# Seven products for eight in 24 pairs of feed-forward weight blocks, with two ring slots split by one instruction there

## The reference, cut to what matters

```python
x = x + (jax.nn.silu(hf @ w_gate[layer]) * (hf @ w_up[layer])) @ w_down[layer]
...
h2 = rms_norm_2(x, g_ffn[i])
x = x + (jax.nn.silu(h2 @ w_gate[i]) * (h2 @ w_up[i])) @ w_down[i]
```

## Time and profile before

| | |
|---|---|
| median of 3 runs | 2388.45 us (2387.97 to 2388.83) |
| the profiled execution: its time / its span | 2390.59 us / 2388.8 us |
| busy: TensorE, VectorE, ScalarE, GpSimd | 100%, 72%, 48%, 1% of the span |
| granted TensorE clock, mean | 0.999 |
| DMA engines | 58.9% of 16 engines' span, 193 GB/s |

### The profile page before, as it was taken

How to read it: one execution, slowest core, us unless ns; L and a number is a source line. 1 busy time by engine, 2 the same in 40 slices (tenths; PEclk the granted TensorE clock), 3 DMA queues, 4 the chain that set the end, 5 groups by cost and what they waited for, 6 DMA issues and landing times.

```text
span 2388.8 us, 31593 instructions
## 1 busy us (share of the span) xinstructions
PE 2380.6 (100%) x10836; PEld 1983.8 (83%) x10836; DVE 1727.6 (72%) x2386; ACT 1145.1 (48%) x1561; POOL 12.8 (1%) x26
## 2 busy tenths in 40 slices
PE   9999999999999999999999999999999999999999
PEld 7988888888888888888888888888888888888887
DVE  7798887876567656668897977977656765666885
ACT  6554555644444434445554445454444443444553
POOL 1000000000000000000000000000000000000000
PEclk9999999999999999999999999999999999999999
DMA  8655555556565665556555564565655565565655
GB/s 294 240 176 185 167 168 175 187 188 207 189 198 178 208 194 189 198 177 196 187 191 200 180 213 161 193 202 187 208 188 199 178 209 193 189 197 180 206 191 168
DMA packets 126859, 461.97 MB, mean 193 GB/s; under 512 B 14096, under 2 KB 14736, under 8 KB 126112
## 3 DMA queue, kind: packets, MB, share of 16 engines
q1 hardware_dynamic: 123648, 446.49, 56.7%
q0 software_dynamic: 2816, 13.68, 1.7%
q10 hardware_dynamic: 288, 0.33, 0.0%
HBM read 458.35 MB, written 2.10 MB: 193 GB/s over the span
## 4 chain that ended last, share of the span: by engine, by line
PE 99%; ACT 0%; DMA 0%; DVE 0%; issue 0%; SPq 0%; DVEq 0%
PE acc L479 94%; PE acc L758 1%; PE acc L484 1%; PE po L741 1%; PE acc L672 1%; PE po L733 1%; PE pt L712 0%; PE acc L687 0%; PE acc L516 0%; PE pt L568 0%; DMA heads<-mem_in 0%; PE acc L657 0%; PE acc L694 0%; ACT tmp_a L1084 0%; PE po L516 0%; ACT tmp_b L1084 0%
## 5 line engine op out<-in xcount | busy, mean ns | idle before, releaser
L1364 DVE TENSOR_TENSOR w_lo<-raw,w_hi 128x1024 fp32r<-128x1024 f32 x844 | 1025.7, 1224 | 580.5 <-ACT w_hi L913 573.0
L913 ACT ACTIVATE w_hi<-raw 128x1024 fp32r<-128x1024 f32 x843 | 890.3, 1060 | 1028.7 <-PE acc L479 951.7
L479 PE MATMUL acc<-w_hi,norm_hi 128*128 128x512 f32 (+1 forms) x2228 | 867.2, 389 | 0.1
L479 PE MATMUL acc<-w_hi,norm_lo 128*128 128x512 f32 (+1 forms) x2228 | 864.0, 388 | 0.0
L479 PE MATMUL acc<-w_lo,norm_hi 128*128 128x512 f32 (+1 forms) x2228 | 592.7, 388 | 0.0
L479 PEld LDWEIGHTS acc<-w_hi,norm_hi 128*128 128x128 f32 x2228 | 418.3, 188 | 85.8 <-issue 0.8
L479 PEld LDWEIGHTS acc<-w_hi,norm_lo 128*128 128x128 f32 x2228 | 418.3, 188 | 85.0
L479 PEld LDWEIGHTS acc<-w_lo,norm_hi 128*128 128x128 f32 x2228 | 417.1, 188 | 85.8
L479 PE MATMUL acc<-w_hi,mix_hi 128*128 128x512 f32 x1088 | 424.7, 390 | 1.9 <-ACT w_hi L1162 1.9
L479 PE MATMUL acc<-w_hi,mix_lo 128*128 128x512 f32 x1088 | 423.8, 390 | 0.0
L479 PE MATMUL acc<-w_lo,mix_hi 128*128 128x512 f32 x1088 | 291.6, 390 | 0.0
(11 more groups left out here) (235 smaller groups left out, 912.9 us busy)
## 6 DMA issues: line engine op xcount, KB each, us to landing
raw<-stream SPq DMA_DIRECT2D x843, 512.0 KB, 4.2
heads<-x_in POOLq DMA_DIRECT2D x4, 512.0 KB, 9.2
x<-x_tok POOLq DMA_DIRECT2D x4, 512.0 KB, 7.4
x<-mem_tok POOLq DMA_DIRECT2D x2, 1024.0 KB, 6.9
x<-x_tok POOLq DMA_DIRECT2D x1, 2048.0 KB, 9.7
heads<-rows_in POOLq DMA_DIRECT2D x2, 1024.0 KB, 8.4
heads<-decay_in POOLq DMA_DIRECT2D x4, 512.0 KB, 5.2
heads<-mem_in SPq DMA_DIRECT2D x3, 512.0 KB, 7.4
```

The source lines that it names most:

```text
L479: last = pe.matmul(acc[:, slot, c * NB:c * NB + width], a[:, k * T + c * P:k * T + (c + 1) * P], w[:, s, kk * width:(kk + 1) * width], sta ...
L913: act.activation(w_hi[:, (units.fixed - 1) % RING, :], src, ACT.Copy).then_inc(w_hi_ready, 1)
L1364: dve.tensor_tensor(w_lo[:, s, :], src, w_hi[:, s, :].bitcast(F32), ALU.subtract)\
```

## The change

In a 2 x 2 product of tiles (two chunks of the contraction by two token tiles, times two chunks by two blocks of columns) seven tile products and some sums take the place of eight (Winograd's form). The change does this for the **first unit of each of the two blocks** of a pair, in 12 pairs of each network: up pair 3 of group 1, all up pairs of groups 2 and 3, the second down pair of group 1, both of group 2. The pairs are numbered j = 0 to 11 in this order of work: group 1: up 3 (0), down 2 (1); group 2: up 1 to 4 (2 to 5), down 1, 2 (6, 7); group 3: up 1 to 4 (8 to 11). The two units leave the stream (48 of 844) and come instead as one 1 MB transfer each from `seven_in`, issued by GpSimd into `heads`.

- VectorE makes three combined weight tiles and one more (`seven_sums`, four subtractions of 512 columns, two of which are waited for), ScalarE rounds four and then three tiles (`seven_hi`, 2048 and 1536 columns), VectorE writes their low parts (`seven_lo`).
- TensorE runs four of the products (`open_seven`, 12 matmuls) inside the second block of the pair before, and three (`close_seven`, 9 matmuls) at the start of the pair; then 7 units per block where there were 8 (5 for 6, 7 for 8 in down pairs). Between the two ScalarE copies one quarter out (`first_out`) and one back (`third_in`), and VectorE adds quarters in PSUM (`combine`, four additions of 512 columns).
- The same sums of activation tiles are made once per network for `norm` and once per group for `mix` (`sums_raw`, `sums_hi`, `sums_lo`).
- For a pair with seven products two blocks use PSUM of `pt` and `po` in some pairs (`banks_at`).
- In `mlp`, outside the last group's down pairs, VectorE's `split` takes two neighbouring slots in one instruction (`split_two`) where the first is even and no other work stands between.
- The hardware loops are written out.

```diff
+            def split_two():
+                raws.add(2)
+                dve.wait_ge(w_hi_ready, units.add(2))
+                s = (units.fixed - 2) % RING
+                dst, src, hi = (t[:, s:s + 2, :].rearrange("p s n -> p (s n)") for t in (w_lo, raw, w_hi))
+                dve.tensor_tensor(dst, src, hi.bitcast(F32), ALU.subtract).then_inc(raw_read, 2)
...
+            def seven_hi(j, part):
+                first, n = ((W11, 4), (W22, 3))[part]
+                if part == 0:
+                    act.wait_ge(seven_summed, j + 1)
+                act.activation(hi7(first, n), raw7(first, n), ACT.Copy).then_inc(seven_hi_ready, 1)
...
+            def open_seven(j, act, ready):
+                c11, c12, c21, c22 = quarters_of(j)
+                pe.wait_ge(block_taken, first_of(j) - 2)
+                pe.wait_ge(seven_ready, 2 * j + 1)
+                pe.wait_ge(act_ready, sums_needed(j))
+                products(j, ((c11, "a11", W11), (c22, "s1", T1), (c12, "s2", T2), (c21, "s3", T3)), act, ready, True)\
+                    .then_inc(products_done, 1)
+            def close_seven(j, act, ready):
+                c11, c12, c21, c22 = quarters_of(j)
+                pe.wait_ge(seven_ready, 2 * j + 2)
+                pe.wait_ge(combined, j + 1)
+                pe.wait_ge(third_copied, j + 1)
+                products(j, ((c11, "a21", W21), (c12, "s4", W22), (c21, "a22", T4)), act, ready, False)\
+                    .then_inc(seven_used, 1)
...
+            def seven_sums(j):
+                dve.wait_ge(seven_landed, 16 * (j + 1))
+                dve.tensor_tensor(raw7(T3), raw7(W22), raw7(T1), ALU.subtract)
+                link(dve.tensor_tensor(raw7(T1), raw7(T1), raw7(W11), ALU.subtract))
+                link(dve.tensor_tensor(raw7(T2), raw7(W22), raw7(T1), ALU.subtract))
+                dve.tensor_tensor(raw7(T4), raw7(W21), raw7(T2), ALU.subtract).then_inc(seven_summed, 1)
...
+            def combine(j):
+                c11, c12, c21, c22 = quarters_of(j)
+                dve.wait_ge(first_copied, j + 1)
+                link(dve.tensor_tensor(u_second, u_first, c12, ALU.add))
+                dve.tensor_tensor(u_third, u_second, c21, ALU.add).then_inc(third_summed, 1)
+                dve.tensor_tensor(c12, u_second, c22, ALU.add)
+                dve.wait_ge(third_summed, j + 1)
+                dve.tensor_tensor(c22, u_third, c22, ALU.add).then_inc(combined, 1)
...
+            for j in range(N_SEVEN):
+                if j:
+                    pool.wait_ge(seven_used, j)
+                else:
+                    pool.wait_ge(w_used, U_MLP_AT[0] + 2)
+                load_seven(j)
```

More of the change, by code:

```diff
@@ new lines, in mlp @@
+                    for p in range(n):
+                        pair = g, "up", p
+                        j, after = (seventh(which, q) for q in all_pairs[all_pairs.index(pair):][:2])
+                        early = {4: [lambda: hidden_hi(p - 1)]} if p else {}
+                        if (g, p) == (0, 0):
+                            during(2 * NU - 3, at)
+                            wait_rows()
+                            gated()
+                            split(3)
+                            taken.add()
+                            continue
+                        if j is None:
+                            sums = {5: [lambda: sums_hi(which, False)], NU - 1: [gated]}
+                            steps(2 * NU, both(early, sums, preparing(after, 6), joining(after, 13)))
+                        else:
+                            sums = {10: [lambda: sums_hi(which, True)]} if p == 2 and g < LAST_GROUP else {}
+                            if after is None and g < LAST_GROUP:
+                                after_ = seventh(which, (g, "down", 1))
+                                ready_ = {}
+                            else:
+                                after_, ready_ = after, joining(after, 11)
+                            steps(2 * NU - 2, both(early, preparing(after_, 5), {NU - 2: [gated]}, sums, ready_))
+                        taken.add()
@@ new lines, in mlp @@
+                    if g == LAST_GROUP:
+                        break
+                    for p in range(2):
+                        pair = g, "down", p
+                        j, after = (seventh(which, q) for q in all_pairs[all_pairs.index(pair):][:2])
+                        turned_ = {3 if j is not None else 4: [lambda: hidden_hi(n - 1)]} if p == 0 else {}
+                        if j is None:
+                            steps(2 * nd, both(turned_, joining(after, 9)))
+                        else:
+                            steps(2 * nd - 2, both(turned_, preparing(after, 6 if p == 0 else 5),
+                                                   joining(after, 2 * nd - 5 if nd > 6 else 9)))
+                        taken.add(2)
@@ L1342, in _ @@
         def _(dve):
-            raws, units, ends, taken, his, squared, sums, roots_n, funcs, rows, own, evicted, roped, moved = (
-                Tally() for _ in range(14))
+            raws, units, ends, taken, his, squared, sums, roots_n, funcs, rows, own, evicted, roped, moved, sums_made = (
+                Tally() for _ in range(15))
             def link(ins):
@@ new lines, in mlp, with steps, preparing, joining @@
+            def mlp(name, next_name, at, which, final=False, beside=None):
+                all_pairs = list(FIRST_BLOCK)
+                def steps(n, then):
+                    by_two[0] = True
+                    done = 0
+                    for at_ in [*sorted(then), n]:
+                        split(at_ - done)
+                        done = at_
+                        for do in then.get(at_, ()):
+                            do()
+                    by_two[0] = False
+                def preparing(j, at):
+                    if j is None:
+                        return {}
+                    return {at: [lambda: seven_sums(j)], at + 3: [lambda: seven_lo(j, 0)],
+                            at + 4: [lambda: seven_lo(j, 1)]}
+                def joining(j, at):
+                    return {} if j is None else {at: [lambda: combine(j)]}
+                def both(*parts):
+                    out_ = {}
+                    for part in parts:
+                        for k, do in part.items():
+                            out_[k] = out_.get(k, []) + do
+                    return out_
@@ new lines, in mlp @@
+                for b in range(NBD):
+                    if b:
+                        if final:
+                            dve.wait_ge(final_ready, b)
+                        rows_ = by_tile(block_of(heads, Y // CB + b - 1)) if final else x_of(b - 1)
+                        for quarter in range(4):
+                            split(1)
+                            turned = turn_quarters(tmp_c[:, :], by_row(rows_), (quarter,))
+                        turned.then_inc(x_turned, 1)
+                        if beside and b == NBD - 1:
+                            beside()
```

479 lines of the change are left out of this document (320 added, 159 removed).

## The result

| | before | after |
|---|---|---|
| time, median | 2388.64 us (2387.97 to 2389.14) | 2427.45 us (2425.69 to 2428.85) |
| ratio to before, 95% interval | | 1.0162 (1.0145 to 1.018) |
| matmuls | 10836 | 10764 |
| TensorE / VectorE busy | 100% / 72% | 98% / 77% |
| network 1, network 2 (TensorE's units, first to last) | 732 / 922 us | 751 / 942 us |

The account below looks back on a forecast made before the run. TensorE, busy 2380.6 of 2388.8 us, was taken as the bound. From the profiled execution, 2390.59 - 16.3 (matmuls saved) + 45 (new waits) = 2419.3, or 2417 us as a median; range 2386 to 2440.

Parts of the forecast that it names:

- What is saved: TensorE, 24 pairs with 21 matmuls where there were 24: 72 x 0.2267 = 16.3 us less, median 2372.1 with no new wait.
- The opening in a common pair: Before `open_seven`, TensorE waits for `seven_lo` 1.20 us, 1.35 with the weight load, at five pairs per network.
- The closing: Before `close_seven`, TensorE waits for `combine` 0.76 us, 0.91 with the load, at seven pairs per network.
- The uncommon places: Three per network: opening of j = 2 waits 4.36 us, its closing 2.55, opening of j = 7 2.5.
- The sum of the waits: All openings, closings and uncommon places: TensorE waits 22.5 us per network, 45 us for both.
- The price of the pieces: Added VectorE and ScalarE instructions, priced from profile rows: `seven_sums` 2.72 us, `combine` 2.63, `seven_hi` 1.84 and 1.40, `seven_lo` 2.22.
- the likeliest case: TensorE's waits as worked out around the products, with their bounds: median 2401 to 2433 us, chance 0.65.
- The rival with the clock: TensorE falls to its lower clock behind six long waits: up to 10 us more, 2427; chance 0.13 together with a late load.
- The rival of the late load: `seven_in` lands over 15.5 us after issue, delaying 14 openings: 3 us late is 2459; chance 0.13 together with lower clock.
- The rival that the added work fits: Added VectorE and ScalarE pieces fit between TensorE's fixed points: 2379 if 40% shorter, 2372 with no waits; chance 0.16.
- What would show it: TensorE idle per network 12 to 16 us before `open_seven`, about 9 before `close_seven`; ScalarE waiting at `seven_hi`; VectorE about 80% busy.

Follow-up runs that it names:

- experiment 1: The change with VectorE's low halves made one slot at a time again, seven products kept: 2403.73 us, ratio 1.0069 to the kernel before.
- experiment 3: The change with one slot per instruction only in the low-half steps directly ahead of `combine`: 2412.54 us, ratio 1.0106 to the kernel before.
- experiment 8: The kernel of experiment 7 with the two-slot low halves put back: 2396.54 us, ratio 1.0034 to the kernel before.
- experiment 2: The change with the opening products one unit later in up pairs that themselves go by seven products: 2415.88 us, ratio 1.0113 to the kernel before.
- experiment 4: The change with sums of weights, first-quarter copy and combination one slot earlier in the second pair of group 1's down projection: 2410.79 us, ratio 1.0093.
- experiment 5: The change with four more linked subtractions of 512 columns on VectorE ahead of each preparation of weights: 2516.26 us, ratio 1.0536 to the kernel before.
- experiment 7: The change with the edits of experiment 1, experiment 2 and experiment 4 together: 2375.20 us, ratio 0.9947 to the kernel before.
- experiment 10: The kernel of experiment 7 with the three products of each tile in another order, first two matmuls sharing an operand: 2374.57 us, ratio 0.9941.
- experiment 9: The kernel of experiment 7 with one or two TensorE waits less ahead of each group of products: 2375.42 us, ratio 0.9948.

## Why the prediction was right, point by point

- **What is saved.** 72 matmuls less (10836 to 10764) at 0.2267 us. The kernels with next to no waits (0.8 and 2.2 us) take 2373.15 and 2375.20 us where 2372.1 was worked out for none.
- **The opening in a common pair.** Forecast 1.35 us, five per network; measured 1.36 ten times over, 1.20 of it idle, at the places that were named. The 0.15 us that I took for the weight load is 0.16.
- **The closing.** Forecast 0.91, seven per network; measured 0.90, at the seven places that were named. That the wide split ahead of `combine` causes it was argued there and is shown by experiments 1, 3 and 8.
- **The uncommon places.** j = 2: forecast 4.36 and 2.55, measured 4.61 and 4.27 (networks 1 and 2), and 2.48. j = 7: 2.5, measured 2.40.
- **The sum of the waits.** 45 us forecast, 44.9 measured.
- **The price of the pieces.** `seven_lo` 2.28 us, of which the next instruction saw 2.20 (710.30 to 712.50), forecast 2.22; `seven_hi` 1.83 (702.78 to 704.61), forecast 1.84. For the 0.11 us until TensorE sees the result of `seven_lo` the prediction gave no row; here its weight load begins 0.16 us after 712.50.
- **Mis-sized: what a wait brings along.** The median came out 10 us higher than 2417. The term that was too small is the price of a wait in the sum, its length and the first weight load alone. The late second matmuls are 2.7 us. The lower clock is 6.5 us; I had it as a rival with up to 10 us and left it out of the likeliest case. It did come, three times in six, and for two openings it is 2.4 and 2.5 us, more than the 1.6 that I took from the program's start. About 1 us is left. The likeliest case's own bounds, 2401 to 2433, hold all the same. The 2.1 us by which the profiled execution of before lay above its median belong ahead of the change: its first network began at 428.11 us, that of after at 425.92.
- **The rival with the clock.** The rule of the Trainium skill, "TensorE: Matmul & The Clock Gate", section "What's actually happening", that an array which has been idle is throttled to half rate and comes back after sustained work, agrees with the rows at 623 to 633 us: 0.50 behind 4.45 us of idle time, then 1.00. It was worth 6.5 us here. That this rival's 2427 us are the measured time is luck: it had a tail behind all six long waits and nothing for the second matmuls; three had one.
- **The rival of the late load.** Not seen: 6.8 us to land in the median and 11.3 at most, with VectorE 76% busy. The Trainium skill, "SBUF — State Buffer", section "SBUF: two separate sides", says that GpSimd cannot write the descriptors of its DMAs while VectorE runs an instruction in a two-port mode. No run here shows in which mode VectorE's instructions ran, so these loads speak neither for that rule nor against it.
- **The rival that the added work fits.** Wrong as it stood: its condition was that the added pieces are 20% or more shorter, and they last as priced. What the experiments show is something else, that the same pieces at full length fit in other places: 2375.2 us with three edits of placement, where 2372 had been forecast for no wait at all.
- **What would show it.** Idle time ahead of `open_seven` 12.5 us per network (forecast 12 to 16), ahead of `close_seven` 7.5 (about 9). VectorE is busy for 76% in the networks where I said 80. The profile put the openings down to "issue" and not to `seven_lo`; the timeline was needed for that.

## What to carry to other kernels

Before new work goes beside a busy engine, count each of its pieces from the point that frees its input to the point where it is wanted, and not in shares of busy time: here VectorE at 77% made TensorE wait for 45 us, and at 80%, with the same seven-product work in other places and single-slot splits, for 2. An instruction that does two steps at once is free only where nothing wanted stands behind it; the same wide step cost nothing in one kernel and over 20 us in another. Price a wait with what follows it: 0.16 us for the broken overlap, 0.08 for the second matmul behind it, and, for a long one, matmuls at the lower clock.

## What the runs showed of the hardware that I had not expected

- **Waits and the granted clock.** Over eight of these traces (after, experiments 1 to 5, 7 and 8), the granted clock in the 2 us behind a wait in front of the products was below full in 20 of 20 cases where TensorE had idled for 3.9 to 7.0 us, in 7 of 22 where it had idled for 2.1 to 3.0 us, and in none of 128 with 0.4 to 1.3 us. The middle case is not decided by the length alone: in experiment 1 the two networks have the same opening with the same 2.97 us of idle time, one at 0.50 behind it and one at 1.00. What decides it wasn't found.
- **At the lower level a matmul of 512 columns started 0.43 us after the one before** (625.57 to 626.00 us in after), against 0.2267.
- **The second matmul behind a wait is 0.08 us late**, 0.31 us after the first in place of 0.23, also when both have the same 128x128 operand (experiment 10) and with fewer waits in front (experiment 9).
